# A two-layer hybrid decoder step: prompt sparse attention computed in pairs of heads

## What is computed

```
h = x + W_out [ SB(xn) | RET(xn) | NSA(xn) ]      xn = RMSNorm(x)
y = h + W_down relu(RMSNorm(h) W_up)^2
```

```
p = softmax(where(vmask, q @ kcmp / 8, NEG));  o_cmp = p @ vcmp
s2 = where(m2, q @ k_selected / 8, NEG);       o_slc = softmax(s2) @ v_selected
s  = where(m, q @ k_window / 8, NEG);          o_win = softmax(s) @ v_window
o_nsa = sum over the branches of gate * o      (a gate per head and branch)
out = concat(o_sb, o_ret, o_nsa) @ W_out
```

## Time and profile before

| | us |
|---|---|
| median of 3 runs | 2365.66 (2365.00 to 2365.71) |
| profiled execution, own time | 2361.28 |
| its span | 2359.5 |
| PE busy | 2147.5 (91%), mean granted clock 0.921 |
| DVE busy | 621.7 (26%) |
| ACT busy | 403.4 (17%) |
| POOL busy | 293.9 (12%) |
| L1220, L1248, L1231 busy, both layers | 125.1, 100.7, 75.9 |

### The profile page before, as it was taken

How to read it: one execution, slowest core, us unless ns; L and a number is a source line. 1 busy time by engine, 2 the same in 40 slices (tenths; PEclk the granted TensorE clock), 3 DMA queues, 4 the chain that set the end, 5 groups by cost and what they waited for, 6 DMA issues and landing times. The chain is left out here.

```text
span 2359.5 us, 25562 instructions
## 1 busy us (share of the span) xinstructions
PE 2147.5 (91%) x10456; PEld 1707.1 (72%) x10456; DVE 621.7 (26%) x1290; ACT 403.4 (17%) x846; POOL 293.9 (12%) x434
## 2 busy tenths in 40 slices
PE   3999878899998999999959997798999799999997
PEld 2888654465687888888858885554657688888886
DVE  1025335944312010000020542478442211000000
ACT  1122342221211000000021224322112200000000
POOL 0005003715000000000000230146130000000000
PEclk9999878969798999999979998798797899999998
DMA  5211302516213222222032203135270312222210
GB/s 172 72 36 37 108 20 89 214 60 242 75 52 126 72 72 72 72 72 72 1 124 72 72 8 100 55 110 211 72 246 4 124 55 74 90 87 72 72 36 37
DMA packets 102230, 203.90 MB, mean 86 GB/s; under 512 B 25760, under 2 KB 34512, under 8 KB 97632
## 3 DMA queue, kind: packets, MB, share of 16 engines
q1 hardware_dynamic: 88288, 135.12, 17.1%
q0 software_dynamic: 13824, 67.12, 7.9%
HBM read 193.53 MB, written 17.06 MB: 89 GB/s over the span
## 5 line engine op out<-in xcount | busy, mean ns | idle before, releaser
L1918 PE MATMUL ps<-xt,ring 128*128 128x260 f32 x2048 | 452.4, 384 | 1.5 <-DVE xt L528 1.5
L1962 PE MATMUL ps<-big,ring 128*128 128x260 f32 x2048 | 449.5, 382 | 0.0
L1918 PEld LDWEIGHTS ps<-xt,ring 128*128 128x128 f32 x2048 | 391.1, 191 | 62.1 <-DVE xt L528 1.6
L1962 PEld LDWEIGHTS ps<-big,ring 128*128 128x128 f32 x2048 | 389.0, 190 | 59.6
L624 PE MATMUL ps<-xt,ring 128*128 128x260 f32 x1536 | 347.8, 385 | 1.5 <-DVE xt L528 1.5
L624 PEld LDWEIGHTS ps<-xt,ring 128*128 128x128 f32 x1536 | 290.4, 191 | 45.7 <-DVE xt L528 1.7
L1935 DVE TENSOR_TENSOR big<-scr 128x520 f32<-128x520 f32 x64 | 44.8, 700 | 410.5 <-ACT scr L1928 410.5
L1279 ACT ACTIVATE xt<-ps,small 128x512 f32<-128x512 f32 (+3 forms) x128 | 67.5, 527 | 393.2 <-DVE small L1303 361.9
L1992 DVE TENSOR_TENSOR x_res<-x_res,ps 128x512 f32<-128x512 f32 x16 | 10.8, 673 | 445.1 <-PE ps L1974 445.1
L1220 PE MATMUL ps<-tt 64*128 64x512 f32 (+3 forms) x256 | 125.1, 577 | 0.0
L783 POOL TENSOR_TENSOR big<-big,scr 128x128 f32<-128x128 f32 (+1 forms) x30 | 15.0, 499 | 875.9 <-DVE scr L738 874.3
(11 more groups left out here) (315 smaller groups left out, 2166.8 us busy)
## 6 DMA issues: line engine op xcount, KB each, us to landing
ring<-in_w_up SPq DMA_DIRECT2D x16, 2048.0 KB, 8.7
ring<-in_w_down SPq DMA_DIRECT2D x16, 2048.0 KB, 7.9
ring<-in_w_in SPq DMA_DIRECT2D x12, 2048.0 KB, 9.1
ring<-in_state_win_k SPq DMA_DIRECT2D x2, 2048.0 KB, 8.4
ring<-in_state_win_v SPq DMA_DIRECT2D x2, 2048.0 KB, 13.8
ring<-in_w_out SPq DMA_DIRECT2D x4, 1024.0 KB, 5.7
ring<-in_w_out SPq DMA_DIRECT2D x8, 512.0 KB, 8.0
out_s_win_k<-in_state_win_k SPq DMA_DIRECT2D x2, 2044.0 KB
```

The costliest lines, as they stand in the source:

```text
L1918: ins = pe.matmul(self.ps[:, 2 * (u % 4) + half, 0:H], w[:, k, f * P:(f + 1) * P], self.xtv[:, k, half * H:(half + 1) * H], start=(k == 0) ...
L1962: ins = pe.matmul(self.ps[:, 2 * f + half, 0:H], w[:, k, f * P:(f + 1) * P], self.hid[:, q * 8 + k, half * H:(half + 1) * H], start=(q == ...
```

## The change

The prompt's units become pairs: pair r of a branch is heads r and r+4, one of each key group, so a tile has one compressed unit, four selected pairs and four window pairs, 36 units in all. Each unit has two `yield`s, and thus two sample steps.

- Scores: the two heads' keys lie in partitions 0 to 63 and 64 to 127, so their products use the two row halves of the array, into banks 0 and 1. One DVE maximum, with the sign turned, covers both banks; ACT exponentiates each. Scores of unit u now wait for the exponentials of unit u-1 (before, of u-2), as there is one pair of banks.
- Scaling: DVE takes the reciprocal of the two sums and multiplies the exponentials, in place in SBUF, by it and by the gate: one instruction per head (L1351 of the new kernel).
- Value products are turned round: 64 value columns are stationary, 128 columns of transposed probabilities stream; the two heads write the two column halves of bank 3, and all three branches add up there. The group closings are gone; ACT copies the finished bank once per tile into `tt`, with features as rows.
- The output projection transposes only the four blocks that are not NSA's and reads NSA's from `tt`.
- `prob` and `pt` lie in columns of `pj`, and the compressed values' layout is ordered (r g d).

```diff
-        prob = [self.xt[:, 0:512], self.xt[:, 512:1024]]
-        pt = [self.xt[:, 1024:1536], self.xt[:, 1536:2048]]
+        prob = [[pj[:, 2 * i + g, R_K:R_K + 512] for g in range(2)] for i in range(2)]
+        pt = [[pj[:, 2 * i + g, N_Q:N_Q + 512] for g in range(2)] for i in range(2)]
...
+        units = [(qt, br, r) for qt in (3, 2, 1, 0) for br in range(3) for r in ((None,) if br == 0 else range(4))]
...
+                    for b in range(qt + 1):
+                        for g in range(2):
+                            ins = pe.matmul(self.ps[g * HD:(g + 1) * HD, 3, r * P:(r + 1) * P],
+                                            pj[:, b, v0 + g * HD:v0 + (g + 1) * HD],
+                                            pt[w % 2][g][:, b * P:(b + 1) * P], start=False,
+                                            stop=(br == 2 and b == qt), skip_group_check=True)
...
-                    if u >= 2:
-                        pe.wait_ge(exp_done, u - 1)
+                    if u >= 1:
+                        pe.wait_ge(exp_done, exps(u - 1))
...
+                        for g in range(2):
+                            p = slice(g * HD, (g + 1) * HD)
+                            ins = pe.matmul(self.ps[:, g, 0:nk], self.tt[p, T_NQ + r, qt * P:(qt + 1) * P],
+                                            self.tt[p, (T_SK, T_WK)[br - 1], 0:nk], start=False, stop=True,
+                                            skip_group_check=True)
...
                 if u >= 2:
...
+                    products(u - 2)
                 yield
+                if 1 <= u <= U and turns[u - 1] == 2:
+                    turn(u - 1, 1)
+                yield
...
+                        dve.tensor_reduce(nmax[u % 2], self.ps[:, 0:2, 0:(qt + 1) * P], AXX, ALU.max, negate=True
+                                          ).then_inc(nmax_ready, 1)
...
+                        inv = rsum[u % 2]
+                        link(dve.reciprocal(inv, inv))
+                        for g in range(2):
+                            x = prob[u % 2][g][:, 0:(qt + 1) * P]
+                            dve.tensor_scalar(x, x, inv[:, g:g + 1], gate(qt, br, r, g), ALU.mult, ALU.mult
+                                              ).then_inc(scaled, 1)
...
+                if u >= 2 and last_of_tile(u - 2):
+                    qt = units[u - 2][0]
+                    act.wait_ge(pv_done, u - 1)
+                    ins = act.activation(self.tt[:, T_NQ:T_NQ + 4, qt * P:(qt + 1) * P],
+                                         self.ps[:, 3, :].rearrange("p (r n) -> p r n", r=4), ACT.Copy)
...
-                for k in range(KD):
-                    ins = pe.transpose(self.ps[:, 2 * (t % 2) + k // 4, (k % 4) * P:(k % 4 + 1) * P],
-                                       pj[:, t, src_cols[k]:src_cols[k] + P], ident)
+                for k in range(4):
+                    ins = pe.transpose(self.ps[:, t, k * P:(k + 1) * P], pj[:, t, src_cols[k]:src_cols[k] + P], ident)
```

More of the change, by code:

```diff
@@ L1182, in prompt_sparse @@
[L1182 to L1195, removed]
@@ new lines, in prompt_sparse, with gate @@
+        units = [(qt, br, r) for qt in (3, 2, 1, 0) for br in range(3) for r in ((None,) if br == 0 else range(4))]
+        U = len(units)
+        turns = [1 if r is None else 2 for _, _, r in units]
+        before = [sum(turns[:u]) for u in range(U + 1)]
+        exps = lambda u: before[u] + turns[u]
+        last_of_tile = lambda u: u % 9 == 8
+        pairs_to = lambda u: sum(1 for x in units[:u + 1] if x[2] is not None)
+        def gate(qt, br, r, g):
+            return self.gates[:, qt, (g * 4 + r) * 3 + br:(g * 4 + r) * 3 + br + 1]
@@ new lines, in pe_steps, with turn, products @@
+        def pe_steps(pe):
+            def turn(w, g):
+                qt, br, r = units[w]
+                pe.wait_ge(scaled, before[w] + g + 1)
+                if g == 1:
+                    pe.wait_ge(copied[0], w + 1)
+                elif w >= 1:
+                    if turns[w - 1] == 2:
+                        pe.wait_ge(copied[1], pairs_to(w - 1))
+                    else:
+                        pe.wait_ge(copied[0], w)
+                for b in range(1 if br == 0 else qt + 1):
+                    ins = pe.transpose(self.ps[:, 2, b * P:(b + 1) * P], prob[w % 2][g][:, b * P:(b + 1) * P],
+                                       self.c("ident"))
+                ins.then_inc(turned, 1)
+            def products(w):
+                qt, br, r = units[w]
+                pe.wait_ge(copied[0], w + 1)
+                if br == 0:
+                    if qt < 3:
+                        pe.wait_ge(o_read, 3 - qt)
+                    for x in range(4):
+                        ins = pe.matmul(self.ps[:, 3, x * P:(x + 1) * P], self.v_diag[:, x * P:(x + 1) * P],
+                                        pt[w % 2][0][:, 0:P],
+                                        start=(x == 0), stop=False, skip_group_check=True)
+                else:
+                    pe.wait_ge(copied[1], pairs_to(w))
+                    v0 = (S_V, W_V)[br - 1]
+                    for b in range(qt + 1):
[4 more added lines that the diff above has]
+                                            stop=(br == 2 and b == qt), skip_group_check=True)
+                ins.then_inc(pv_done, 1)
@@ L1223, in pe_steps @@
                     ins.then_inc(qk_done, 1)
                 if 1 <= u <= U:
[L1225 to L1232, removed]
@@ L1233, in pe_steps @@
-                    ins.then_inc(turned, 1)
-                if u >= 2:
[L1235 to L1250, removed]
+                    turn(u - 1, 0)
@@ L1821, in output_projection @@
             self.freed[IT_WO + n] = ((mm_done, 4 * (n + 1)),)
-        src_cols = [SB_Q, SB_Q + P, R_Q, R_Q + P] + [N_Q + j * P for j in range(4)]
+        src_cols = [SB_Q, SB_Q + P, R_Q, R_Q + P]
+        features = lambda k, h: (self.xtv[:, k, h * H:(h + 1) * H] if k < 4
+                                 else self.tt[:, T_NQ + k - 4, h * H:(h + 1) * H])
         def pe_part(pe):
```

148 lines of the change are left out of this document (65 added, 83 removed).

## The result

The changed kernel takes 2301.39 us (median of 4 runs, 2300.08 to 2301.95), the kernel before 2365.33 beside it: a ratio of 0.9732 (0.9715 to 0.9748). The profiled execution took 2301.21, 60.1 less than that of before.

What follows compares the result with a forecast made beforehand. No single engine bounds the whole: PE bounds stages 1 and 4, DVE stage 2, and stage 3 has a low clock. Terms sum to -14.4 us a layer, -28.8 in all: 2337 us median, range 2308 to 2372.

Steps and rivals of the forecast that it cites:

- stage 2: Sparse attention's cached keys, DVE-bound: +4 us a layer, from scalings waiting for POOL against group closings gone; bounds -6 and +23.
- stage 3: Sparse attention's softmax, at a low clock: pairs replace heads, -7 us a layer, three quarters of 9.2.
- stage 6: Transpositions ahead of W_out: 16 of 34 records go, -2.7 us a layer.
- stage 5: The prompt alone, clock at 0.50: eleven rounds of pairs in series replace sixteen rounds, +3 us a layer.
- stage 1: Sparse attention's window keys, PE-bound: four pairs at 1.42 us less each, -5.7 us a layer; bounds -8 and -2.
- stage 4: Sparse attention's values, PE-bound: eight pairs at 2.23 us in place of 3.10, shaded for gathers to -6 us a layer.
- Sharing: On PE's array, a pair's score products and value products each take 1.19 us, 0.69 of serial time, from column-strip records.
- the rival of serial rows: A pair's score products run one after the other: 13.9 us a layer lost, 2365 us, no change; chance 0.13.
- the rival: In stage 2, DVE's scalings wait out a whole POOL multiplication each period, stage 4 loses its gain: 2377 us; chance 0.14.
- Two signs of being wrong: Scalings of 2 us and more beside POOL's multiplication, and a clock under 0.9 in stage 2, would show the forecast wrong.
- the rival of PE's longer pauses: PE's longer pauses lower its clock in stage 2, costing about 10 us a layer: 2357 us; chance 0.10.
- The rival with the higher clock: Stages 3 and 5 run at 2.4 GHz half their time, about 10 us a layer more gone: 2317; chance 0.12.

Runs made afterwards that it cites:

- the idle-time products: Unread PE products of 384 columns at two softmax-stage waits: added to the changed kernel, 2285.80 us (0.9669); added to the kernel before, 2356.91 us (0.9953).

## Why the prediction was wrong

The direction was right, and so was the sharing of the array; the sum was half of what came. The step that failed is the clock, which every term took as it had been before. Outside stage 2 the low clock cost 12.6 us less in layer 2, and 18.1 less in layer 1. The sum holds some 3 of that (half of stage 3's 7 and a part of stage 6, less half of stage 5's 3). So the clock is about 10 of the 15.9 us missing in layer 2. PE's work outside stage 2 is 4 to 5 of them (20.2 less, where the sum holds some 16), and stage 2 is 1.3. By its steps:

- **The clock in stages 3, 1 and 4** (put at nothing): it changed from 0.61 to 0.71 in stage 3, where the low clock cost 8.0 us less. In stage 1 the low stretch at its start fell from 8.5 us to 5.3, worth 1.6 by the two rows below this list, and stage 4 no longer starts low, worth 2.1. A quarter of stage 3's saving had been struck off because another chain might end last; PE idled only 1.4 us more there. That filling PE's pauses raises this clock, and moves stage 3 by 4 to 6 us in layer 2, the idle-time products showed. But the changed kernel's own two pauses are longer than before (2.46 and 2.94 for 1.92 and 2.44). What raised its clock stays open.
- **Sharing** (1.19 a pair for the scores and for the value products, from strips of columns): right in kind, too small. They take 1.06 and 1.03; the row taken as the nearest was of another kind. The undoing of the row halves cost 16.2 us in layer 2, where the rival of serial rows had put 13.9.
- **What a stage holds** (stages 1 and 4): miscounted. Stage 1 was given the value products of four pairs, and holds those of two (32 records; before 56, seven heads). A round is now two sample steps, so the prompt is further behind at the mark, and the rest runs in stage 2, where PE's time costs nothing. Stage 4 was taken as sixteen heads, but before it holds 18 mask records, for 18 heads (now 16, for eight pairs). Two of them are heads of tile 0, which the forecast had already put into stage 5. One of them takes 1.51 at a clock of 0.50 (1774.25 to 1775.76), so the two are some 1.5 us at 2.4 GHz. The shading for the gathers was wrong too: the stage shortened as PE did, with the DMA share at 0.81.
- **Stage 2** (+4, measured +2.7): near, but by errors that cancel. The scalings wait in six of the stage's seven pairs, 12.3 us in the layer, where 4.9 had been put. But the weightings behind them had waited 6.1 in the layer before and no longer do, which neither the forecast nor the rival took off. The rival's place and price were right and its result wrong. In the value steps of stage 4 scalings wait as well (2.53 in place of 0.41), at no cost, since PE ends last there.
- **Two signs of being wrong** came: scalings above 2 us, and a clock under 0.9 in stage 2 (0.85). The second is the rival of PE's longer pauses. It cost nothing, because DVE's list ended last: PE idled 19.4 of the 81.6 us.
- **Stage 5** (+3, measured +1.2) and **stage 6** (-2.7): near, and right. Stage 5 ran at 0.57 in place of 0.50.
- **The rival with the higher clock** (2317, 0.12) put 10 us a layer on stages 3 and 5; there the low clock cost 9.0 less in layer 2 and 13.6 in layer 1. It was given too little, because it was argued down by the amount of PE's work.

The start of stage 1 before, and then after, by stretch:

```profile
1522.10:1530.60 8.50, 8.50 (x16) 3.31 (x17) 2.43 (x6) 1.27 (x3) 4.54 (x2) 0.50 0.29 115
```

```profile
1492.70:1498.00 5.30, 5.30 (x13) 1.84 (x13) 0.96 (x1) 0.00 (x0) 4.54 (x2) 0.50 0.47 186
```

A part of the shorter low-clock time is only less work in low stretches. In stage 3 PE's work fell by 14% (31.0 to 26.8) and the cost of the low clock by 39% (20.7 to 12.7). So by an estimate that keeps the low share, some 2.8 of the 8.0 us are less work and the rest is a higher grant.

## What to carry to other kernels

Count the units that each stage really holds, by the records of one line in it, before pricing them by stage, and price a period by the mean of all of them. Here two fp32 products on the two row halves of the array, into two banks, took the time of one; two heads of 64 are worth issuing together. Where a stage's granted clock is 0.5 to 0.7 behind a pause of PE, try products that fill the pause: here they shortened stage 3 in every kernel. But look at the whole time as well: it fell by 16 us in one kernel and rose by 7 in another, whose clock was lower elsewhere.

## What was not expected of the hardware

A DVE operation on two columns lasts 2.33 us while POOL multiplies, a scaling of 512 columns 2.60 in place of 0.54, whether its columns are contiguous or in steps of two; the one-input reciprocal L1317 passed in 0.19. A scaling with one tensor input waits like an operation with two, a reciprocal with one does not; what tells these apart was not tried further. Who waits is not settled by the starts alone: in stage 4 the scalings start 0.04 us ahead of POOL's multiplication in the trace and wait all the same, while a weighting 0.16 ahead makes POOL wait. Sixteen value records take 1.03 with the column halves in turns and 1.51 with one half after the other, in which order some still overlap. Four score records take 1.06 on two row halves and 1.91 on one: 45% less.
